# Block products for the branch projections beside a chunked state-space scan: 32 weight tiles as 16 pairs of 2x2 block products

## The reference

```
h = rmsnorm(x, norm_pre)
xbc, dt_raw, z_ssd, sc_h, sc_b, sc_c, z_sc = split(h @ w_in)       # z_ssd .. z_sc: 1024 columns each
xbc = silu(causal_dwconv(xbc, ssd_conv_w, ssd_conv_b))             # 4 taps; 1280 channels: xs, B, C
y_ssd = ssd_chunked(xs, softplus(dt_raw + dt_bias), -exp(a_log), B, C, d_skip)   # chunks of 128 tokens
y_ssd = rmsnorm(y_ssd * silu(z_ssd)) * ssd_norm                    # over 2 groups of 512 channels
y_sc = sc_b * causal_dwconv(sc_c * sc_h, sc_conv_w) * silu(z_sc)   # 3 taps
x = x + rmsnorm(concat(y_ssd, y_sc) @ w_out, norm_post)
```

## Time and profile before

| | us |
|---|---|
| median of 3 runs | 2522.97 (2521.09 to 2523.66) |
| the profiled execution | 2525.81 |
| its span | 2524.1 |
| PE busy | 2427.9 (96%) |
| DVE busy | 1480.8 (59%) |
| POOL busy | 1048.4 (42%) |
| ACT busy | 739.1 (29%) |

### The profile page before, as it was taken

How to read it: one execution, slowest core, us unless ns; L and a number is a source line. 1 busy time by engine, 2 the same in 40 slices (tenths; PEclk the granted TensorE clock), 3 DMA queues, 4 the chain that set the end, 5 groups by cost and what they waited for, 6 DMA issues and landing times.

```text
span 2524.1 us, 34217 instructions
## 1 busy us (share of the span) xinstructions
PE 2427.9 (96%) x12962; PEld 1987.8 (79%) x12962; DVE 1480.8 (59%) x1930; ACT 739.1 (29%) x947; POOL 1048.4 (42%) x560
## 2 busy tenths in 40 slices
PE   7999999999999899999999999999989999899995
PEld 6777888887888678777878788788877888788885
DVE  7765556556521473113156766745788666777788
ACT  4332222222200221243022232222254333343443
POOL 4433343334344453333223223233464555466661
PEclk9999999999999999999999999999999999999998
DMA  5121222213111322122222222222134444843321
GB/s 203 44 67 67 66 83 72 78 58 117 34 50 50 100 92 85 42 96 82 81 77 74 78 68 76 78 81 90 58 110 150 147 168 145 307 187 136 129 100 67
DMA packets 100936, 245.62 MB, mean 97 GB/s; under 512 B 10849, under 2 KB 36705, under 8 KB 96242
## 3 DMA queue, kind: packets, MB, share of 16 engines
q1 hardware_dynamic: 59904, 186.67, 22.3%
q10 hardware_dynamic: 40946, 57.78, 6.8%
HBM read 183.53 MB, written 60.88 MB: 97 GB/s over the span
## 4 chain that ended last, share of the span: by engine, by line
PE 80%; DVE 9%; issue 4%; DMA 2%; ACT 2%; POOL 2%; ACTq 0%; DVEq 0%; SPq 0%; POOLq 0%
PE pt L2024 47%; PE pt L2419 14%; PE wk L2419 6%; PE pt L2040 1%; PE pt L2054 1%; DMA eb<-o_d 1%; PE wk L2325 1%; PE wk L2430 1%; PE wk L2181 1%; PE pt L2122 1%; PE wk L2182 1%; PE wk L2295 1%; DVE eb L1688 1%; PE wk L2360 1%; PE wk L2359 1%
## 5 line engine op out<-in xcount | busy, mean ns | idle before, releaser
L545 POOL TENSOR_TENSOR w_hi<-w_raw,ones 128x1024 fp32r<-128x1024 f32 x137 | 264.5, 1931 | 1116.1 <-PE pt L2024 1064.0
L549 POOL TENSOR_TENSOR w_lo<-w_raw,w_hi 128x1024 fp32r<-128x1024 f32 x138 | 381.6, 2765 | 12.5 <-ACT w_hi L662 1.7
L2024 PE MATMUL pt<-xh,w_hi 128*128 128x512 f32 x960 | 299.9, 394 | 2.5 <-ACT ea L795 2.5
L2024 PE MATMUL pt<-xh,w_lo 128*128 128x512 f32 x960 | 297.4, 391 | 0.0
L2024 PE MATMUL pt<-h,w_hi 128*128 128x512 f32 x896 | 290.9, 406 | 1.8 <-ACT cu_o L907 1.8
L2024 PE MATMUL pt<-l,w_hi 128*128 128x512 f32 x896 | 278.0, 392 | 0.0
L2024 PE MATMUL pt<-h,w_lo 128*128 128x512 f32 x896 | 277.1, 390 | 0.0
L2024 PE MATMUL pt<-xl,w_hi 128*128 128x512 f32 x848 | 262.8, 391 | 0.0
L2024 PEld LDWEIGHTS pt<-xh,w_hi 128*128 128x128 f32 x960 | 179.6, 189 | 47.2 <-issue 10.1
L2024 PEld LDWEIGHTS pt<-xh,w_lo 128*128 128x128 f32 x960 | 181.2, 189 | 38.2
L2024 PEld LDWEIGHTS pt<-l,w_hi 128*128 128x128 f32 x896 | 168.8, 188 | 36.7
(11 more groups left out here) (521 smaller groups left out, 5069.4 us busy)
## 6 DMA issues: line engine op xcount, KB each, us to landing
w_raw<-ws_d SPq DMA_DIRECT2D x140, 512.0 KB, 3.6
fx_d<-stg SPq DMA_DIRECT2D x106, 256.0 KB, 2.8
fraw<-ws_d SPq DMA_DIRECT2D x32, 512.0 KB, 5.0
raw<-ws_d SPq DMA_DIRECT2D x32, 512.0 KB, 8.2
xs0f<-fx_d SPq DMA_DIRECT2D x10, 1024.0 KB, 4.9
xs1f<-fx_d SPq DMA_DIRECT2D x9, 1024.0 KB, 4.8
xs2f<-fx_d SPq DMA_DIRECT2D x9, 1024.0 KB, 4.9
x_raw<-xT_d SPq DMA_DIRECT2D x32, 256.0 KB, 7.4
```

The source lines that it names most:

```text
L545: nc.gpsimd.tensor_tensor(out=w_hi[:, u, :], in0=w_raw[:, u, :], in1=zeros, op=ALU.add).then_inc(w_hi_done, 1)
L549: nc.gpsimd.tensor_tensor(out=w_lo[:, u, :], in0=w_raw[:, u, :], in1=w_hi[:, u, :].bitcast(f32), op=ALU.subtract).then_inc(w_split, 1)
L2024: ins = MM(pt[:, slot, h * HALF:(h + 1) * HALF], wt[:, k * P:(k + 1) * P], x[:, k, h * HALF:(h + 1) * HALF], start=first and k == 0 and n ...
```

## The change

Eight tiles each of four projections become 16 pairs: (sc_c, sc_h) and (z_ssd, z_sc) of one channel tile. A pair is a 2x2 block product (two tiles x two halves of the 1024 inputs, two halves of the tokens) made of seven products in place of eight (`sc_product`, 12 matmuls each, 14 per chunk), in the order `SC_ORDER = (1, 6, 7, 5, 4, 2, 3)`. What that takes:

- Differences of the normalised input's blocks, made once: 16 subtractions on DVE (`differences`), roundings on ACT, rests on POOL (`thi`, `tlo`), all inside the xbc stage.
- Sums of weight blocks, per pair: two on DVE (`weight_sums`), two on POOL (`third_sum`, `fourth_sum`). The high part of each factor is made by ACT (`sc_hi`), the low part by POOL (`sc_lo`). Four weight slots, which lie in the places of `xh` and `xl` of rows 0 to 3, second half of the tokens. That part of the input is stored to `x12_d` before, and loaded back after the last product.
- Sums of products, per pair: two copies on ACT (`sc_first`, `sc_11`), five additions on DVE (`part_u2`, `part_x`, `part_22`, `part_21`, `part_12`). The gates and the sc_c x sc_h product are made by halves of 512 tokens (`gate_z`, `gate_branch`, `product_half`).
- `xbc`, the scan's output and the branch go to DRAM (`xbc_d`, `ys_d`, `sv_d`) and are loaded when needed; the chunk is loaded by SP (`chunk_load`) and no longer staged by ACT.
- ACT makes the last tap of the first convolution out of PSUM (`xbc_copy`), the first tap of the second (`first_tap`), the 16 decay rows (`decay_rows`, with relu), and the high part of the weight tiles of the later xbc tiles.
- The last two xbc tiles are made by halves of the tokens, second half first. In the first chunk the scan's parts come after products 6 and 12, in the others after 1 and 8.
- The first two sc_b tiles have their own places, and their second half over rows 0 to 3 waits for the reload. Loads for the gating are issued by SP as the gated products go on; the square of tile i runs beside the product of tile i + 1, in two buffers.

The core of the diff (the helper functions that only wrap one instruction, the places in memory and the shifted semaphore counts are left out):

```diff
+    def sc_slot(g):
+        return xh[:, g % 4, cols(1)], xl[:, g % 4, cols(1)]
...
+        for j in range(C):
+            n = 2 * j
+            if j < C - 1:
+                sp.wait_ge(sw_lo, 7 * n + 7)
+                sc_load(n + 2)
+            sp.wait_ge(y_evac, j + 1)
+            sp.dma_start(ys_d.rearrange("i p t -> p i t")[:, :, j * P:(j + 1) * P], yb[:]).then_inc(ys_put, 16)
+            if j < C - 1:
+                chunk_load(j + 1)
+                sp.wait_ge(sw_lo, 7 * n + 14)
+                sc_load(n + 3)
+            else:
+                sp.wait_ge(ssd_b, C)
+                sp.wait_ge(sw_lo, 7 * n + 7)
+                sp.dma_start(sb0_raw[:], ws[S_SB + 4 * C, :, :]).then_inc(sc_in[0], 16)
+                sp.dma_start(sb1_raw[:], ws[S_SB + 4 * C + 1, :, :]).then_inc(sc_in[1], 16)
...
+                for u in range(2):
+                    sp.sem_inc(w_loaded[u], 16)
+                    sp.dma_start(w_raw[:, u, :], ws[S_SB + 4 * C + 2 + u, :, :]).then_inc(w_loaded[u], 16)
+            sp.wait_ge(sz_done, 2 * j + 2)
+            sp.dma_start(sz_d[j, :, :], szb[:].rearrange("p h n -> p (h n)")).then_inc(sz_put, 16)
...
+        def v_load(i):
+            sp.dma_start(vbuf[:, i, :], sv_d[i, :, :]).then_inc(x_in[1][i], 16)
+        sp.wait_ge(ys_put, 16 * C)
+        sp.wait_ge(sc_prod, SC_PRODUCTS - 2)
+        y_load(0)
+        sp.wait_ge(w_split, S_SB + 2)
+        sp.dma_start(acc_a[:], sz_d[1, :, :]).then_inc(sz_in[1], 16)
+        y_load(1)
+        sp.wait_ge(sc_prod, SC_PRODUCTS)
+        for n, x in enumerate((xh, xl)):
+            sp.dma_start(x[:, 0:4, cols(1)].bitcast(f32), x12_d[n, :, :, :]).then_inc(x12_in, 16)
+        y_load(2)
+        sp.wait_ge(v_done, 3 * C)
+        sp.dma_start(sv_d[C - 1, :, :], vj[:]).then_inc(sv_put, 16)
+        sp.wait_ge(sv_put, 16 * (C - 1))
+        for i in range(3, KT):
+            sp.wait_ge(yz_done, i - 2)
+            y_load(i)
...
+        pool.wait_ge(y_evac, C)
+        for u, raw in enumerate((sb0_raw, sb1_raw)):
+            pool.wait_ge(sc_in[u], B_SIN)
+            zeros = ones[:, 1:2].to_broadcast([P, 1024])
+            if u:
+                pool.wait_ge(ys_put, 16 * C)
+                pool.wait_ge(sz_put, 16 * C)
+            nc.gpsimd.tensor_tensor(out=sb_h[u][:], in0=raw[:], in1=zeros, op=ALU.add).then_inc(w_hi_done, 1)
+            pool.wait_ge(w_hi_done, S_SB + u + 1)
+            nc.gpsimd.tensor_tensor(out=sb_l[u][:], in0=raw[:], in1=sb_h[u][:].bitcast(f32), op=ALU.subtract).then_inc(w_split, 1)
+        pool.wait_ge(v_done, 3 * C)
+        for u in range(2):
+            split(u, 16 * (S_SB // 2 + 2))
+            rest(u, S_SB + 3 + u)
+        split_pairs(S_SB // 2 + 2, S_GATE // 2)
...
+        def xbc_copy(j, u):
+            act.wait_ge(mm_done, j * 2 + (S_XBC + u + 1))
+            act.wait_ge(conv_done, j * 2)
+            A(raw_p[:, u, CW - 1:CW - 1 + T], pt[:, u, :], ACT.Copy)
+            if j:
+                act.wait_ge(silu_done, 2 * j)
+            A(conv_o[:, u, :], pt[:, u, :], ACT.Identity, scale=V("conv_w", j * 2 + u + (CW - 1) * XBC_T),
+              bias=V("conv_b", j * 2 + u)).then_inc(evac_done, 1)
+            n = S_XBC + 2 * j + u + 2
+            if n < S_SB:
...
+        def sc_hi(g):
+            n, i = divmod(g, 7)
+            p = SC_ORDER[i]
+            if g >= 4:
+                act.wait_ge(sc_prod, g - 3)
+            if p in (1, 2, 4):
+                act.wait_ge(sc_in[n % 2], 32 * (n // 2 + 1))
+            elif p in (5, 6):
+                act.wait_ge(sw_sum, 2 * n + p - 4)
+            else:
+                act.wait_ge(sw_sum2, 2 * n + (1 if p == 7 else 2))
+            A(sc_slot(g)[0], sc_factor(n, p), ACT.Copy).then_inc(sw_hi, 1)
...
+        def tanh(j, m):
+            n = 2 * j + 1
+            if m == 2:
+                act.wait_ge(sz_done, 2 * j + 1)
+            else:
+                act.wait_ge(sc_part, 5 * n + (3, 4, 0, 5)[m])
+                if m == 3:
+                    act.wait_ge(sz_done, 2 * j + 2)
+                elif j:
+                    act.wait_ge(v_done, 3 * j)
+            A(th[:, m % 2, :], (s22[:], sx5[:], bank(0), su2[:])[m], ACT.Tanh, scale=0.5).then_inc(sc_th, 1)
+        def first_tap(j):
...
+        for j in range(1, C):
+            a, b = 14 * j, 14 * j + 7
+            last = j == C - 1
+            sc_hi(a + 3)
+            sc_first(2 * j)
+            if j > 1:
+                decay_exp(j)
+            sc_hi(a + 4)
+            sc_hi(a + 5)
+            if j == 1:
+                in_decay(j)
+            state_rows(j)
+            sc_hi(a + 6)
+            if j == 1:
+                decay_rows(j, 0, 8)
+            sc_hi(a + 7)
+            if j == 1:
+                decay_rows(j, 8, HEADS)
+                decay_exp(j)
+            sc_hi(a + 8)
+            sc_11(2 * j)
+            sc_hi(a + 9)
+            sc_hi(b + 3)
+            sc_first(2 * j + 1)
+            first_tap(j)
+            sc_hi(b + 4)
+            sc_hi(b + 5)
+            if not last:
+                rows_load(j + 1)
+            sc_hi(b + 6)
+            tanh(j, 0)
+            if not last:
+                sc_hi(b + 7)
+                in_decay(j + 1)
+            tanh(j, 1)
+            if not last:
+                sc_hi(b + 8)
+            sc_11(2 * j + 1)
+            tanh(j, 2)
+            if not last:
+                decay_rows(j + 1, 0, 8)
+                sc_hi(b + 9)
+                decay_rows(j + 1, 8, HEADS)
+            tanh(j, 3)
...
+        act.wait_ge(sv_put, 16 * C)
+        act.wait_ge(sz_put, 16 * C)
+        act.dma_start(eb[:], sz_d[2, :, :]).then_inc(sz_in[0], 16)
         def gated(i):
-            if i + 1 < KT:
-                if i:
-                    act.wait_ge(yz_done, i)
-                act.dma_start((ec if i % 2 == 0 else eb)[:], sz_d[i + 1, :, :]).then_inc(sz_in[(i + 1) % 2], 16)
             act.wait_ge(yz_done, i + 1)
-            act.wait_ge(sq_used, KT + i)
-            A(acc_b[:], xbc[:, i, :], ACT.Square).then_inc(sq_done, 1)
+            if 1 <= i and i + 2 < KT:
+                act.dma_start((eb if i % 2 == 0 else ec)[:], sz_d[i + 2, :, :]).then_inc(sz_in[i % 2], 16)
...
+        def weight_sums(n):
+            r, sums = sraw[n % 2], ssum[n % 2]
+            dve.wait_ge(sc_in[n % 2], 32 * (n // 2 + 1))
+            if n >= 2:
+                dve.wait_ge(sw_lo, 7 * n - 10)
+            TT(out=sums[:, 0, :], in0=r[:, 1, 0, :], in1=r[:, 1, 1, :], op=ALU.add).then_inc(sw_sum, 1)
+            dve.wait_ge(sw_sum, 2 * n + 1)
+            TT(out=sums[:, 1, :], in0=sums[:, 0, :], in1=r[:, 0, 0, :], op=ALU.subtract).then_inc(sw_sum, 1)
...
+        def part_x(n):
+            j, b = divmod(n, 2)
+            dve.wait_ge(sc_prod, 7 * n + 3)
+            dve.wait_ge(sc_part, 5 * n + 1)
+            if n:
...
+        for j in range(1, C):
+            a, b = 2 * j, 2 * j + 1
+            part_u2(a)
+            weight_sums(b)
+            scan_input(j)
+            part_x(a)
+            scan_decayed(j)
+            part_22(a)
+            scan_c(j)
+            part_21(a)
+            scan_matrix(j)
+            product_half(j, 0)
+            part_12(a)
+            product_half(j, 1)
+            tap(j, 1)
+            part_u2(b)
+            tap(j, 2)
+            if j < C - 1:
+                weight_sums(b + 1)
+            scan_out(j)
+            part_x(b)
+            scan_state(j)
+            part_22(b)
+            gate_z(j, 1)
+            part_21(b)
+            gate_z(j, 0)
+            gate_branch(j, 0)
+            part_12(b)
...
+        gated(0)
+        for i in range(1, 6):
             gated(i)
-            if i in (3, 5):
-                branch((i - 3) // 2)
-        for i in range(2, 4):
-            branch(i)
+            add_squares(i - 1)
+        add_squares(5)
+        branch(0)
+        gated(6)
+        gated(7)
...
+        def sc_product(g):
+            n, i = divmod(g, 7)
+            p = SC_ORDER[i]
+            out = bank((0, 1, 3, 2, 3, 0, 2)[i])
+            pe.wait_ge(sw_lo, g + 1)
+            if n == 0 and i < 4:
+                pe.wait_ge(evac_done, N_SB - 1 if i < 2 else N_SB)
+            elif i == 0:
+                pe.wait_ge(sc_t1, 2 * n)
+                if n > 1:
+                    pe.wait_ge(sc_th, (n // 2 - 1) * 4 + 3)
+            elif i < 4:
+                pe.wait_ge(sc_part, 5 * (n - 1) + (1, 4, 5)[i - 1])
+            elif i == 5:
+                pe.wait_ge(sc_t1, 2 * n + 1)
+            else:
+                pe.wait_ge(sc_part, 5 * n + (2 if i == 4 else 3))
+            w = sc_slot(g)
+            for k in range(4):
+                x = sc_operand(p, k)
+                for m, (wt, xx) in enumerate(((w[0], x[0]), (w[0], x[1]), (w[1], x[0]))):
+                    ins = MM(out, wt[:, k * P:(k + 1) * P], xx, start=i < 4 and k == 0 and m == 0, stop=k == 3 and m == 2, skip_group_check=True)
+            ins.then_inc(sc_prod, 1)
+        def scan_first(j):
...
```

(21 more changed lines are left out.)

586 lines of the change are left out of this document (427 added, 159 removed).

## The result

The changed kernel takes 2496.5 us as a median (2493.7 to 2499.2, four runs) against 2522.0 (2517.8 to 2523.7) for the one before on the same chip: ratio 0.9907, 95% interval 0.9891 to 0.9923. The forecast was 2485, its range 2453 to 2506. The profiled execution's span is 2496.8 us, 27.3 less than before; from the first product of the mixer on, both kernels are alike to 1 us.

What follows compares the result with a forecast made beforehand. TensorE was taken as the bound, busy nearly the whole span. Terms -30.8 (seven chunks), -14.5 (first chunk), +3.5 (convolution), +3.5 (gating) sum to -38.3: 2487.5 us profiled, 2485 us median, chance 0.47; range 2453 to 2506.

Steps and rivals of the forecast that it cites:

- first product: Convolution stage: eight differences ahead of conv_pair(2) delay tile 10's weights, so PE waits: +3.5 us (0 to 8).
- first chunk: First chunk of the loop: 46.2 us instead of 60.7, with 1.8 us of waits: -14.5 us.
- seven chunks: Other chunks of the loop: 45.6 us each instead of 50.0, of which 1.2 us collision waits: -30.8 us.
- gating stage: sc_b tiles with gating: 94.5 us of work, 13.5 of wait, 2.2 of lower clock, 110.2 in all: +3.5 us.
- rival 3: Gating: reloads one by one, 5.1 us per gated step instead of 2.9, some 5 before the sums: 2497 us; chance 0.08.
- rival 5: Loop: block products miss the matmul pitch, each waiting for its weights, 0.3 us x 112: 2519 us; chance 0.04.
- the chain of ACT: Chunk tail from part_22 through tanh 0, in_decay, tanh 1 to tanh 2: 6.5 us, leaving product 0 0.3 us slack.
- the prediction's own sign: Loop: PE waits before product 0 point to tanh; if they stand before products 4 or 11, it was part_x.
- rival 2: Loop: DVE and POOL collide more, chunk 48 us: 2504 us; chance 0.15.
- rival 4: Loop: DVE becomes the bound, each of 20 two-operand operations waiting a whole POOL operation, 61 us a chunk: 2608 us; chance 0.04.
- it just fits: Gating: x12 lands at 16.1 us after the last product, PE wants it at 16.4.
- 4.2 MB up to and with the store: Gating: SP's queued transfers, ending with sv_d[7]'s store, take 12.2 us plus 2.4 latency and delay ACT's first square.

Runs made afterwards that it cites:

- experiment 12: Changed kernel with the edits of experiment 10, experiment 9 and experiment 8, later differences and part_x(0) ahead of memsets and weight_sums(1): 2478.1 us, ratio 0.9829.
- experiment 7: Changed kernel with ACT making in_decay after tanh 2 instead of before tanh 1: 2502.5 us, ratio 0.9930 against the kernel before.
- experiment 8: Changed kernel with the second pair's weight sums after part_x of the first pair (chunks 1 to 7): 2502.4 us, ratio 0.9931.
- experiment 9: Changed kernel with the next chunk's first-pair weight sums moved from before scan_out to behind part_21(b): 2499.3 us, ratio 0.9914.
- experiment 5: Changed kernel with DVE taking conv_pair(2) before the last eight differences; ACT's roundings and POOL's rests follow: 2496.5 us, ratio 0.9895.
- experiment 3: Changed kernel with the first sc_b bank's copy and branch(0) after gated(3), not gated(5): 2504.8 us, ratio 0.9935.
- experiment 4: Changed kernel with only the first sc_b bank's copy after gated(3), rounding and branch(0) left behind gated(5): 2497.9 us, ratio 0.9906.
- experiment 10: Changed kernel with x12 and store issued first, sz_d[3] loaded with the first square, bank copies earlier, sums and spreads one tile later: 2484.9 us, ratio 0.9862.

## Why the prediction was right, and where it was not

Step by step, in us against the forecast's own terms: first product +5.0 (forecast +3.5), first chunk -11.0 (-14.5), seven chunks -29.6 (-30.8), gating stage +9.0 (+3.5): together -26.6 against -38.3, and the span fell by 27.3. The gating stage is half of the miss, the first chunk most of the rest. The time is that of rival 3, 2497, but its mechanism did not come: gated(2) to gated(5) started 3.1 us apart in the mean (565.05 to 574.24, three steps) and not 5.1, and no wait stood before the sums. Nor did another rival come true.

- *The loop.* Right: 320.4 us against 319.2 (7 x 45.6). The products keep the pitch of the earlier trace rows, and rival 5 is out. PE's own work is about 44.6 us and not 44.4: at each of three joins of products with scan matmuls one start comes 0.1 us late (experiment 12's 44.74 still hold 0.2 before product 0). The waits are therefore 0.9 us, not 1.2. Of them 0.3 stand before product 0, released by tanh 2, and the chain of ACT ran as written (it ended 0.15 us before product 0). The larger part, 0.6, stands before product 4: by the prediction's own sign, `part_x`. That the chunk came out within 0.1 us of the forecast is in part luck: more work of PE, fewer waits, and most of them in another place. The step stopped the chain at tanh 2, where it goes on through the decay rows, tanh 3 and gate_branch (experiments 7, 8, 12).
- *Collisions.* DVE was counted at 30 us a chunk and is busy 37 (259.5 / 7): 7 us more, of which no more than the 0.9 us of waits reach PE. The weight sums near 2 us (1.66) spoke for rivals 2 and 4, but these needed a chunk of 48 or 50.4. Rival 4 fell by its own measure: it decides from a mean wait of 1.0 us for each of the 20 two-operand operations, and 7 us over 20 are 0.35. L1709 takes 0.97 us more than the 0.69 it has alone (experiment 9), each time; all 70 additions with an operand in PSUM took 0.68 to 0.69 us, so that the ten sums a chunk that PE waits for most directly were never hit. By the Trainium skill ("SBUF — State Buffer", "SBUF: two separate sides") the exclusive port is taken by a DVE operation with two SBUF inputs, against a GpSimd operation that reads SBUF, as POOL's here do, and the loser blocks. The trace agrees: sums with two such inputs were held up, those with one in PSUM never.
- *The first chunk.* Its waits are 1.3 us (product 4) and 2.0 (reload), where 1.8 were taken. `part_x(0)` stands behind the last convolution and two weight sums, which the step never walked through. Another 1.7 us are the lower clock behind the reload's wait, a term that the step left out: some eight starts 0.43 us apart instead of 0.23, granted clock 0.83 from 190 to 200. In all 49.7 instead of 46.2.
- *The convolution stage.* The wait at tile 10 is 3.6 us, released by POOL, as forecast; the 1.4 beyond it fit the granted clock of 0.71 in the 5.5 us behind the wait (144.5 to 150.0), where before it was 1.00. Experiment 5 shows the cause that the step gave, the eight differences.
- *The gating stage.* The mechanism held: the squares start at TS + 22.3 (19), and from SP's first issue to the store's landing it is 14.3 us, where 14.6 were counted. The wait for the copy is 13.3 us (13.5), but that nearness is luck: the copy ended at TS + 39.9 instead of 35.4, and PE came for it at TS + 26.7 instead of 21.9. Mis-sized were three terms. The split of sb1 ends at TS + 7.6 instead of 4.5: it waits for the sz store to land, which took 2.86 us from TS - 0.2, while the step leaves, from TS - 0.6 on, little more than the split's own 4.8. So x12 landed at TS + 19.4 and cost 3.0 us where "it just fits" was written. And the lower clock cost 5.2 us where 2.2 were taken: 1.8 behind the wait for x12, and 3.4 in two tiles of 12.6 us each instead of 10.9. The cause that the prediction gave, 4.2 MB up to and with the store, is only half of it: with the store first the copy came 4.3 us sooner, and with x12 first too 6.8; the rest went only with an earlier load of sz_d[3] and another order together (experiment 10), since the order alone gained nothing (experiments 3, 4).
